# Signalling a split weight block in halves: GpSimd releases, and TensorE waits for, four weight tiles at a time

## What is computed

```python
proj = h @ w_in[l]
mix_out = merged @ w_out[l]
f = jnp.square(jax.nn.relu(h @ w_ff1[l])) @ w_ff2[l]
```

## Time and profile before

| | |
|---|---|
| Runs | 3365.08 us median (3363.25 to 3367.71) |
| Profiled execution, its time | 3367.82 us |
| Its span (first to last instruction) | 3365.9 us |
| TensorE matmul busy | 3213.8 us (95%), 19314 matmuls |
| GpSimd busy | 1961.7 us (58%) |
| VectorE, ScalarE busy | 1709.9 us (51%), 1068.2 us (32%) |
| Weight loads from HBM | 434 of 512 KB, median 3.5 us from issue to landing |

### The profile page before, as it was taken

How to read it: one execution, slowest core, us unless ns; L and a number is a source line. 1 busy time by engine, 2 the same in 40 slices (tenths; PEclk the granted TensorE clock), 3 DMA queues, 4 the chain that set the end, 5 groups by cost and what they waited for, 6 DMA issues and landing times.

```text
span 3365.9 us, 53885 instructions
## 1 busy us (share of the span) xinstructions
PE 3213.8 (95%) x19314; PEld 2514.2 (75%) x19314; DVE 1709.9 (51%) x2741; ACT 1068.2 (32%) x1988; POOL 1961.7 (58%) x2607
## 2 busy tenths in 40 slices
PE   7998999999999999899999999999999999999998
PEld 4766777777877887577777778877667778777887
DVE  4456777754444344633645544445551634555345
ACT  2153443431211113543534311113551536231112
POOL 4623333336588874245455788875336374888786
PEclk8999999999999999999999999999999999999999
DMA  5341111112222222012122222222112121222222
GB/s 206 145 156 45 45 39 45 33 39 97 75 94 94 94 96 62 32 51 75 51 70 70 88 94 94 94 94 79 41 32 94 43 84 46 93 88 95 94 94 94
DMA packets 70794, 265.22 MB, mean 79 GB/s; under 512 B 7744, under 2 KB 7872, under 8 KB 67520
## 3 DMA queue, kind: packets, MB, share of 16 engines
q1 hardware_dynamic: 68288, 257.59, 22.7%
q10 hardware_dynamic: 2304, 4.83, 0.4%
HBM read 260.29 MB, written 2.10 MB: 78 GB/s over the span
## 4 chain that ended last, share of the span: by engine, by line
PE 72%; POOL 10%; DVE 7%; issue 5%; ACT 4%; DMA 1%; SPq 0%; POOLq 0%; DVEq 0%; ACTq 0%
PE psum_a L579 9%; PE psum_a L582 8%; PE psum_a L583 8%; POOL w_lo L3383 7%; PE psum_d L579 6%; PE psum_d L583 6%; PE psum_d L582 6%; PE psum_d L645 5%; PE psum_a L737 3%; POOL w_hi L3378 2%; PE psum_d L840 2%; PE psum_a L767 2%; PE psum_a L771 1%; PE psum_a L770 1%; PE psum_d L1211 1%
## 5 line engine op out<-in xcount | busy, mean ns | idle before, releaser
L3383 POOL TENSOR_TENSOR w_lo<-raw,w_hi 128x256 fp32r<-128x256 f32 x1736 | 1422.0, 850 | 36.2
L3377 POOL TENSOR_TENSOR mark<-mark 128x1 f32<-128x1 f32 x432 | 95.1, 220 | 1322.1 <-PE psum_a L579 662.5
L579 PE MATMUL psum_a<-h_hi,w_hi 128*128 128x512 f32 x1600 | 640.5, 400 | 7.6 <-POOL w_lo L3383 6.8
L582 PE MATMUL psum_a<-h_lo,w_hi 128*128 128x512 f32 x1600 | 625.6, 391 | 0.0
L583 PE MATMUL psum_a<-h_hi,w_lo 128*128 128x512 f32 x1600 | 625.6, 391 | 0.0
L3378 POOL TENSOR_SCALAR w_hi<-raw 128x1024 fp32r<-128x1024 f32 x434 | 461.5, 1063 | 33.6 <-DMA raw<-in_weights 33.6
L579 PEld LDWEIGHTS psum_a<-h_hi,w_hi 128*128 128x128 f32 x1600 | 301.8, 189 | 101.1 <-POOL w_lo L3383 22.7
L583 PEld LDWEIGHTS psum_a<-h_hi,w_lo 128*128 128x128 f32 x1600 | 301.6, 188 | 64.8
L582 PEld LDWEIGHTS psum_a<-h_lo,w_hi 128*128 128x128 f32 x1600 | 302.0, 189 | 61.5 <-issue 2.2
L579 PE MATMUL psum_d<-split,w_hi 128*128 128x512 f32 x848 | 334.2, 394 | 4.8 <-POOL w_lo L3383 4.4
L583 PE MATMUL psum_d<-split,w_lo 128*128 128x512 f32 x848 | 330.3, 390 | 0.0
(11 more groups left out here) (407 smaller groups left out, 5541.1 us busy)
## 6 DMA issues: line engine op xcount, KB each, us to landing
raw<-in_weights SPq DMA_DIRECT2D x434, 512.0 KB, 3.5
plain<-in_ada SPq DMA_DIRECT2D x20, 1024.0 KB, 6.9
arena<-in_ada SPq DMA_DIRECT2D x4, 1024.0 KB, 17.3
x<-in_x SPq DMA_DIRECT2D x1, 2048.0 KB, 12.5
x<-in_x ACTq DMA_DIRECT2D x1, 2048.0 KB, 9.0
out<-x SPq DMA_DIRECT2D x8, 256.0 KB, 3.7
arena<-in_pe ACTq DMA_DIRECT2D x2, 512.0 KB, 3.6
const<-in_const ACTq DMA_DIRECT2D x1, 906.0 KB, 8.5
```

The lines of the kernel that those rows point to most:

```text
L579: m = pe.eng.matmul(dst, wh, hi(t), start=t == 0, stop=False)
L582: pe.eng.matmul(dst, wh, lo(t), start=False, stop=False)
L3377: eng.tensor_tensor(b.mark[:, 1:2], b.mark[:, 0:1], b.mark[:, 0:1], ALU.add)
L3383: m = eng.tensor_tensor(lo[:, part], b.raw[:, s, part], hi[:, part].bitcast(F32), ALU.subtract)
```

## The change

GpSimd raises `w_ready` twice a block, after the second and after the fourth quarter of the low part. TensorE waits at every tile whose number divides by four, so at the first and at the fifth tile of a block, for one count each. SyncE multiplies its own threshold by two, so it still waits for the whole block. The two loops on TensorE count twice as many `w_ready` per turn. When `w_used` is raised, the rings, the instructions of GpSimd and the order of all matmuls stay as they are.

```diff
-TILES = 8
+TILES, PART = 8, 4
...
     def new_block(self):
-        return self.at % TILES == 0
+        return self.at % PART == 0
...
-    with pe.loop(turns, w_ready=24, w_used=24, full_a=16, full_d=16, hid_lo=8):
+    with pe.loop(turns, w_ready=24 * TILES // PART, w_used=24, full_a=16, full_d=16, hid_lo=8):
...
-    with pe.loop(turns, w_ready=16, w_used=16, full_a=8, full_d=16, hid_lo=8):
+    with pe.loop(turns, w_ready=16 * TILES // PART, w_used=16, full_a=8, full_d=16, hid_lo=8):
...
-                        eng.wait_ge(sig["w_ready"], i * RAW + (s + 1 - RAW))
+                        eng.wait_ge(sig["w_ready"], (i * RAW + (s + 1 - RAW)) * (TILES // PART))
...
                 for n in range(4):
                     part = slice(2 * n * P, 2 * (n + 1) * P)
                     m = eng.tensor_tensor(lo[:, part], b.raw[:, s, part], hi[:, part].bitcast(F32), ALU.subtract)
-                m.then_inc(sig["w_ready"], 1)
+                    if n % 2:
+                        m.then_inc(sig["w_ready"], 1)
```

## The result

The changed kernel takes 3304.39 us (median of 4 runs, 3303.44 to 3306.98), against 3365.04 us for the kernel before (median of 4, 3363.25 to 3367.71). The ratio is 0.9821, with a 95% interval from 0.9809 to 0.9833: 60.7 us or 1.8% faster. I had said 3316 us, with a range from 3306 to 3332. What fell short is the sum of what goes: the small delays behind late starts were put at 2 us and are 8, and 4.5 us were taken off for the attention stages that did not come back.

What follows compares the result with a forecast made beforehand. TensorE, 95% busy, loses time at block starts to GpSimd's late splits. Dense 40.4 + recurrence 2.1 + attention 4.5 = 47, and some 2: 49 us; 3367.8 becomes 3319, runs 2.7 lower: 3316 us, range 3306 to 3332.

Steps and rivals of the forecast that it cites:

- the sum of what goes: Gain over all stages: 40.4 us dense, 2.1 recurrence, 4.5 attention, and some 2 for small rests: 49 us.
- some 2 us: First 20 blocks and matmul distances of 0.23 to 0.24 us right after a late start: some 2 us gained.
- the 9.1 us of the attention stages: Loss counted at late block starts in the attention stages between the dense stretches: 9.1 us, half of it taken as gain.
- The bound and the cycle: At block starts, TensorE starts, GpSimd splits, TensorE starts: no room to make up, so a late split delays the next.
- Added waits and the added signal at 0: 434 fifth-tile waits on TensorE and one more GpSimd signal a block: taken as 0 us; bound for the waits 48 us.
- The weight load that is not made ahead: At a late block start, the second matmul comes 0.11 us late; this kind of loss sums to 10.6 us.
- 51.6 us for late starts: 138 late starts in blocks 21 to 433: 41.0 us at first matmuls and 10.6 at second, all offered by the mechanism.
- The 2.1 us that the prediction puts in the recurrence: Loss at late block starts counted for the recurrence stage, taken whole into the gain: 2.1 us.
- Half given back in the attention stages: Waits on VectorE or ScalarE there may take back half of 9.1 us, so 4.5 us is counted as gain.
- Partly given back: Rival, chance 0.16: contention between GpSimd and VectorE grows with the pace; gain only 15 to 35 us, 3330 to 3350 us.
- no change: Rival, chance 0.03: TensorE's wait moves whole from the first to the fifth tile; 3365 us.
- slower: Rival, chance 0.03: new TensorE waits make their weight loads late, 48 to 65 us in all; 3381 us at 0.15 each.

Runs made afterwards that it cites:

- The short split: The kernel before, still one signal a block, with two of GpSimd's four low-part instructions left out, so part of the computation is missing: 3296.60 us, ratio 0.9784.
- three quarters: The changed kernel, with the first signal after the third quarter of the low part and TensorE waiting at the first and seventh tile: 3308.65 us, ratio 0.9826.
- the late release: The changed kernel, with `w_used` raised by the first matmul of the fifth tile instead of the first, half a block later: 3612.63 us, ratio 1.0733.
- The waits alone: The kernel before, with 434 already met fifth-tile waits added on TensorE and GpSimd still signalling once a block: 3365.74 us, ratio 0.9999.

## Where the prediction was right, and the step that failed

The bound and the mechanism were right; the step that failed is the sum of what goes. It had 40.4 + 2.1 + 4.5 and some 2, 49 us. Two of its terms were wrong: "some 2 us" for the first 20 blocks and for the small distances behind a late start, where the recount below has 8, and the 9.1 us of the attention stages of which half was taken off, where the traces show nearly nothing given back. With both put right the prediction's own sum is 59.7 us, which from the median of 3365.1 gives 3305.4 us; measured were 3304.4.

**The bound and the cycle: right.** TensorE was held up at block starts by a split that ended late, and the kernel had no room to catch up. The short split (all of the gain without any half), three quarters (4.0 us of late starts in its trace, by replay 3.4 to 5.4) and the late release (308 us slower than the changed kernel, by replay 335) each agree with that cycle, the last two in their numbers, within a tenth for the release.

**Added waits and the added signal at 0: right.** The waits alone give 0.9999; four signals instead of two give no difference.

**The weight load that is not made ahead, 0.11 us: right.** Taken matmul by matmul, from the first matmul to the last the two profiled executions differ by 63.1 us, of which 40.9 lie at the first matmul of a block and 13.1 at the second. The rule of the Trainium skill (TensorE: Matmul & The Clock Gate, The mechanism), by which loads overlap only across row groups, would have had nothing at the second.

**The size: the term of what goes was too small.** The prediction had 51.6 us for late starts and "some 2 us for the first 20 blocks and for matmul distances of 0.23 to 0.24 us right after a late start". A recount over all blocks, with no threshold above the free distance, gives 144 late starts: 42.5 us at the first matmul, 12.9 at the second and 4.3 behind them, 59.7 us. So 2 us should have been 8. I had seen that the tail could be worth something, and put it at the edge of a case instead of into the sum: the range gives "8 us in all" for the same distances for which the sum has its 2. The 2.1 us that the prediction puts in the recurrence are two starts before it (244.1 and 268.6 us, blocks 21 and 24); the recurrence itself, blocks 30 to 65, has no late start. And beside the four groups of waits that it adds up to 23.5 us the view has two more, of 0.9 and 0.7 us, behind lines 1052 and 631. Neither moves the sum.

**Half given back in the attention stages: wrong.** This step ("I take half") took 4.5 us off without a row for it. In the traces of before and after, outside the stretches at half clock, 9.1 us go at and behind the block starts of the attention stages (blocks 145 to 199 and 286 to 340), and 0.5 us come back at all the other matmuls there. The run with halves in the dense stretches only points the same way: 12.2 us come from elsewhere, where the recount has 13.1. There what was taken from a late start stayed, but for this half microsecond.

**The profiled pair differs by more than the recount, 63.1 instead of 59.7 us, by its clock.** The half-speed clock stood for 82 us in the profiled execution before and 66 us in the one after. Matmuls that began at half clock in the first execution only took 13.8 us longer there, those that did so in the second only took 6.8 us longer there: 6.9 us in favour of the changed kernel. At full clock in both executions the difference is 56.2 us, 3.5 less than the recount, so a small part of the recount came back or was held up by something else as well; what that is stays open. I don't put the clock down to the change, since its share differs from profile to profile without a pattern that I can tie to an edit: the kernel with four signals had 80 us of it, and the recurrence alone had between 0 and 14 us. The medians differ by 60.7 us, 1.0 more than the recount.

**Partly given back, no change, slower:** none came. The low part's mean is 852 ns instead of 850, so the change doesn't set the contention off. The contention itself is real: the kernels with two and with eight low-part instructions are 30 and 19 us slower than the changed one, though with eight GpSimd's larger sum, and with two the clock, has a part in that.

## What to carry to other kernels

If a producer may start only when the consumer starts, compare the producer's slowest turn, not its mean, with the consumer's period: GpSimd, 58% busy, was late 144 times. Signalling in halves adds room at no cost that could be measured here, and the smallest advance that covers most late turns already gives most of the gain. Count a late start by the distances between starts, the ones behind it included, until they are back at the free pace; and don't discount a gain by a feeling, but by a row.

## What the runs showed of the hardware

- A weight load over all 128 rows runs under the matmul before it (it starts 0.01 us after that matmul). One late start costs its wait, 0.09 us in the mean at the second matmul (12.9 us over 144) and 0.03 us spread over the next nine (4.3 us over 144), none of which is more than 6 ns beyond the free 0.227 us in the median.
- A wait on TensorE that is already met costs less than 0.007 us in the mean (434 of them, in unrolled code and in the loops, whose thresholds are in registers: ratio 0.9999, 0.9990 to 1.0008).
- GpSimd's float32 subtraction over 128 partitions takes 0.46, 0.74 and 1.30 us (medians) for 128, 256 and 512 columns: some 0.2 us fixed. Instructions start 0.70 us apart at 256 columns, with or without a signal on the one that ends between them (0.699 us behind the second quarter after the change, 0.698 before).
- GpSimd's instructions show in VectorE's chain, by their length and by their number: the same wait of TensorE for VectorE was 6.6, 11.0 and 15.1 us with 128, 256 and 512 columns, although GpSimd's total fell (1693, 1426 and 1253 us), and 6.9 us with half as many instructions of 256 columns.
